# Expert rows in tiles of 32 tokens by 4 picks, indices and weights moved between partitions by products

## The chip, the cores and the metric

One core of one Trainium2 chip runs the whole program. The metric is device time in microseconds for one execution; less is better. All data is float32.

## The reference, cut to what matters

One layer of a hybrid network over 256 context tokens and 1024 latent tokens, D = 1024. Token mixing (gated MLP, pooling, retention) comes first. The change lies in the channel mixing, which looks up 128 experts for each token (8 heads by 16 picks):

```python
qp = (xt @ wq).reshape(t, PEER_HEADS, 2, PEER_DKEY // 2)
sc = jnp.einsum('thsk,hsnk->thsn', qp, subkeys)
top_s, top_i = lax.top_k(sc, PEER_TOPK)
...
best_s, best_p = lax.top_k(cand_s, PEER_TOPK)
expert = jnp.take_along_axis(cand_i, best_p, axis=-1)
g = jax.nn.softmax(best_s, axis=-1)
act = jax.nn.gelu(jnp.einsum('thkd,td->thk', u_tab[expert], xt))
y = jnp.einsum('thk,thkd->td', g * act, v_tab[expert])
```

Each expert is a row of `u_tab` and one of `v_tab`, 4 KB each, kept side by side in `in_peer` (8 KB). 1280 tokens by 128 picks are 163,840 rows, 1342 MB.

## The kernel before

The tokens are 10 chunks of 128. Two kinds of work are interleaved in one list of events, and each engine runs its part of the list in that order.

*The front* is everything but the expert rows, in stages: the retention scans and the pooling of the context, then of the latents; then, for groups of chunks (0: two, 1: two, 2: three, 3: three), a dense part (projections by weights streamed through the two buffers of `ring`, gates, output projection, the normed input h2) and a ranking part. There each chunk and pair of heads takes one `wq` event (query product, transposes, scores, on PE) and on DVE the events `topa`, `topb`, `topc` for each head of the pair: top 16 of each side, top 16 of the sums, then the expert numbers. The ranking goes pair by pair: pair 0 of every chunk of the group, then pair 1, and so on. Group 0's ranking is spread over the latent scans (two of its events behind each `hq`, `hk`, `hv` event).

*The rows* are 1280 row tiles, 128 for each chunk. A row tile holds 64 tokens by 2 picks on 128 partitions. POOL gathers its 128 rows of 8 KB into one of 8 slots (6 until group 0 is ranked) once the pair's indices are there and the slot is free (`row_free`). DVE multiplies the u half by h2 and sums (L1447), ACT makes the gelu, the weight and the weighted selection `lhs` (L953, L954, L958), PE multiplies `lhs` (64 columns) with the v half, 512 columns into each half of the PSUM partitions (L1178), and the slot is free. Inside a chunk the tiles go pair by pair, 16 of one half of the tokens (`g2`), 16 of the other. `h2R` holds h2 of the 64 tokens twice, for each half of a chunk. After a half's last tile DVE multiplies the sums by the gate (L1531) and adds them to the output rows (L1535).

DVE writes expert numbers and softmax weights straight into the rows' layout: the picks of a token that lies on one partition are spread over two, by 4 small instructions a head for the indices (L1500) and 8 a pair for the weights (L1515).

`Plan.merge` sets the order. It gives every front event a cost (the largest of its PE, ACT and DVE estimates), spreads the 128 tiles of a group's chunks evenly by cost from the point at which that group's rows may start to that of the next group (the last group at one tile for 2.9 us), and puts a tile behind an event when it is due and its pair is ready:

```python
while row + 1 <= due[n + 1] and self.ready[row_of(row)[0], row_of(row)[2]] <= n + 1:
```

What is not placed by the end of the front follows as the tail. PE runs a tile's product three tiles late, ACT one.

## Time and profile before

| | us |
|---|---|
| median of 3 runs | 4936.25 |
| lowest, highest | 4924.78, 4938.27 |
| the profiled execution | 4929.44 |
| its span, first to last instruction | 4927.7 |
| mean granted TensorE clock | 0.847 |

The profiled execution lies 6.8 us under the median, within the runs. The span is read by stage, since the mean shares mix stages with different bounds; the windows below are cut at the last scan update (1075), the last h2 of each group (1653, 2457, 3596) and the last index product of each ranking (1969, 2950, 4105, rounded to the instruction behind it).

### The profile page before, as it was taken

Reading aid. Unit: us, or ns where it says so; the run is one execution under the profiler, and the core shown is the slowest. Engines: PE = TensorE matmul, PEld = TensorE weight load, DVE = VectorE, ACT = ScalarE, POOL = GpSimd, SP = SyncE. Lnnn points to the kernel's source line nnn. Section 1 sums busy time; section 2 is a strip of 40 time slices with the busy share of each in tenths; the row PEclk is TensorE's granted clock in tenths of the full one; section 3 lists DMA queues with packets and bytes.
Section 4 is the critical chain, followed back from the end, with each engine's and each line's share of the span. In section 5 each row is a group of like instructions: output and inputs, shape, how many; then the busy total and the mean of one; then the engine's idle time right before and its main releaser. Section 6 shows DMA issues by size and latency. Waiting matters only on the chain. (4 is left out here: it accounts for less than half of the span.)

```text
span 4927.7 us, 44934 instructions
## 1 busy us (share of the span) xinstructions
PE 3968.5 (81%) x12301; PEld 1584.9 (32%) x12301; DVE 2747.1 (56%) x6701; ACT 1593.8 (32%) x4955; POOL 1616.5 (33%) x1312
## 2 busy tenths in 40 slices
PE   6999898999999865999876658988876755666666
PEld 4644355554434321344321213343322210111110
DVE  1112678433234499455569895545468996544544
ACT  4111244332122243323333333323343333333333
POOL 0000123221122232343333334344333334555554
PEclk8999999999999975999987769999977766666666
DMA  6644787878798987999999899999999878999998
GB/s 252 223 182 176 252 314 290 302 268 333 283 367 342 340 346 272 375 380 380 393 369 351 363 358 369 422 396 384 412 418 370 341 294 347 409 421 415 415 422 354
DMA packets 290059, 1687.33 MB, mean 342 GB/s; under 512 B 29136, under 2 KB 71184, under 8 KB 111120
## 3 DMA queue, kind: packets, MB, share of 16 engines
q0 software_dynamic: 184320, 1342.26, 68.8%
q1 hardware_dynamic: 97472, 318.79, 17.0%
q10 hardware_dynamic: 8016, 23.42, 1.5%
q8 instruction: 98, 1.61, 0.1%
q14 instruction: 153, 1.25, 0.1%
HBM read 1646.57 MB, written 37.78 MB: 342 GB/s over the span
## 5 line engine op out<-in xcount | busy, mean ns | idle before, releaser
L913 POOL DMA_INDIRECT slots<-in_peer,idxR x1280 | 1610.2, 1258 | 3257.8 <-PE ps L1178 2525.8
L1178 PE MATMUL ps<-slots,lhs 128*64 128x512 f32 x5120 | 1667.9, 765 | 818.3 <-ACT lhs L958 815.9
L1447 DVE CUSTOM_DVE_ANT_0 slots<-slots,h2R 128x1024 f32<-128x1024 f32 x1280 | 1540.2, 1224 | 814.8 <-issue 730.1
L1166 PE MATMUL ps<-ring,arena 128*128 128x512 f32 (+1 forms) x3996 | 1591.0, 553 | 28.8 <-DMA ring<-in_wq 22.2
L1166 PEld LDWEIGHTS ps<-ring,arena 128*128 128x128 f32 x3996 | 760.6, 195 | 884.2 <-issue 830.2
L1178 PEld LDWEIGHTS ps<-slots,lhs 128*64 128x64 f32 x5120 | 330.8, 158 | 2018.6 <-ACT lhs L958 1695.3
L953 ACT ACTIVATE gelus<-dots 128x1 f32<-128x1 f32 x1280 | 256.0, 200 | 1596.4 <-DVE dots L1447 1593.8
L958 ACT ACTIVATE lhs<-fold,wgts 128x64 f32<-128x64 f32 x1280 | 445.1, 348 | 41.9
L954 ACT ACTIVATE wgts<-gelus,gsmR 128x1 f32<-128x1 f32 x1280 | 377.1, 295 | 42.1
L1166 PE MATMUL ps<-ring,slots 128*128 128x512 f32 (+1 forms) x704 | 250.9, 518 | 0.4 <-DMA ring<-in_wz 0.4
L1166 PEld LDWEIGHTS ps<-ring,slots 128*128 128x128 f32 x704 | 134.0, 191 | 114.3 <-issue 105.9
L1118 ACT ACTIVATE tmp<-ps 128x512 f32<-128x512 f32 x60 | 35.8, 597 | 318.9 <-PE ps L1166 318.9
L1686 DVE SCALAR_TENSOR_TENSOR tmp<-tmp,ps 128x512 f32<-128x512 f32 x40 | 27.5, 688 | 194.7 <-ACT tmp L1123 194.7
L1166 PE MATMUL ps<-arena,ring 128*128 128x512 f32 x256 | 117.9, 615 | 10.6 <-DMA arena<-hT_scratch 10.6
L1447 DVE DVE_READ_ACCUMULATOR2_ANT dots<- 128x1 f32 x1280 | 104.9, 82 | 0.0
L1641 DVE TENSOR_TENSOR inb<-ps,inb 128x512 f32<-128x512 f32 x20 | 13.8, 691 | 144.6 <-PE ps L1166 139.0
L1667 DVE SCALAR_TENSOR_TENSOR arena<-tmp,arena 128x512 f32<-128x512 f32 x20 | 13.8, 692 | 137.9 <-ACT tmp L1118 137.9
L1123 ACT ACTIVATE tmp<-ps 128x512 f32<-128x512 f32 x40 | 23.9, 597 | 204.2 <-PE ps L1166 204.2
L953 ACT ACT_TABLE_LOAD x58 | 74.4, 1283 | 41.7 <-DVE dots L1447 41.0
L1142 ACT ACTIVATE arena<-ps 128x512 f32<-128x512 f32 x40 | 23.8, 596 | 193.0 <-PE ps L1166 193.0
L1515 DVE TENSOR_SCALAR gsmR<-es,rsum 64x8 f32<-64x8 f32 x320 | 74.2, 232 | 5.5
L1166 PEld LDWEIGHTS ps<-arena,ring 128*128 128x128 f32 x256 | 48.8, 196 | 80.8 <-issue 80.8
(194 smaller groups left out, 2340.4 us busy)
## 6 DMA issues: line engine op xcount, KB each, us to landing
ring<-in_whead SPq DMA_DIRECT2D x24, 2048.0 KB, 9.4
ring<-in_wa SPq DMA_DIRECT2D x24, 2048.0 KB, 9.6
ring<-in_wq SPq DMA_DIRECT2D x16, 2048.0 KB, 18.4
slots<-in_peer,idxR POOLq DMA_INDIRECT x1280, 11.4
ring<-in_wlate SPq DMA_DIRECT2D x16, 1024.0 KB, 7.5
ring<-in_wgc SPq DMA_DIRECT2D x16, 1024.0 KB, 9.4
ring<-in_wgb SPq DMA_DIRECT2D x8, 2048.0 KB, 10.0
ring<-in_wout SPq DMA_DIRECT2D x8, 2048.0 KB, 12.6
```

Source lines behind the costliest of these rows:

```text
L913: g.indirect_dma_start(out=slot(R), out_offset=None, in_=a["peer"], in_offset=bass.IndirectOffsetOnAxis(ap=idxR[:, p % KEEP, g2, col:col + ...
L953: st.link(A_(gelus[:, n:n + 1], dots[:, n:n + 1], ACT.Gelu_apprx_tanh))
L954: st.link(A_(wgts[:, n:n + 1], gelus[:, n:n + 1], ACT.Copy, scale=gsmR[:, p % KEEP, g2, col:col + 1]))
L958: A_(lhs[:, n, :], fold[:, :], ACT.Copy, scale=wgts[:, n:n + 1]).then_inc(s["w_done"], 1)
L1118: A_(tmp[:, ev.x % TMPS, :], bank(t), ACT.Tanh, scale=0.5).then_inc(freed[t % BANKS], 1)
L1123: A_(tmp[:, ev.x % TMPS, :], bank(t), ACT.Tanh, scale=0.5).then_inc(s["gate_done"], 1)
L1142: A_(qp[:, m % 2, :], bank(t), ACT.Copy).then_inc(freed[t % BANKS], 1)
L1166: done = mm(out, lhsT, rhs, start=n == 0, stop=n == len(pairs) - 1)
L1178: done = mm(ps[j * HALF:(j + 1) * HALF, g2, :], lhs[:, R % LHS, :], slot(R)[:, D + j * UW:D + (j + 1) * UW], start=start, stop=stop)
L1447: v.tensor_tensor_reduce(out=u, in0=u, in1=h2R[:, g2, :], scale=1.0, scalar=0.0, op0=ALU.mult, op1=ALU.add, accum_out=dots[:, R % LHS:R % ...
L1515: done = v.tensor_scalar(gsmR[i * HALF:(i + 1) * HALF, p % KEEP, g2, h * 8:h * 8 + 8], es[there, b, hd, :].rearrange("p (q i) -> p i q", i ...
L1686: v.scalar_tensor_tensor(out=gate, in0=gate, scalar=1.0, in1=bank(t), op0=ALU.add, op1=ALU.mult).then_inc(freed[t % BANKS], 1)
```

## The change

A row tile becomes 32 tokens by 4 picks. The product uses four column groups: `lhs` has 32 columns, and each of four products covers 256 columns of v and its own 32 PSUM partitions. The 64 tiles of a chunk's first half (64 tokens, quarters 0 and 1 by turns of 8 tiles) all come before those of the second half (quarters 2 and 3). `h2R` holds h2 of 32 tokens four times, so it is loaded four times for a chunk, and the sums are evacuated four times, by 1 + 4 instructions.

Expert numbers and weights go to a new buffer `vals`, on the partition of their token, by one instruction a head each. A new event `mv` multiplies slices of the identity with `vals` (16 products a pair), which puts every pick on its partition in PSUM; ACT copies the weights into `gsmR`. A new event `mw` lets DVE copy the indices into `idxR`. Only then may POOL gather for the pair. In the list `mv` stands behind the first `topc` of the next pair, `mw` behind the `topa` after that. Both are events of the ranking, so group 0's takes 8 instead of 6 places for a pair.

The planner has a pair ready at its `mw`, takes 2.8 instead of 3.3 us for each `top` event, and lets the rows of groups 2 and 3 start at the first chunk's pair 2 (was pair 1).

```diff
 def row_of(R):
-    p, rr = divmod(R, ROWS)
-    pair, g, qq = rr // 32, rr // 16 % 2, rr % 16
-    return p, g, pair, pair * 16 + qq, 2 * pair + qq // 8
+    p, n = divmod(R, ROWS)
+    g, pair = 2 * (n // HALF) + n // 8 % 2, n // 16 % 4
+    return p, g, pair, 8 * pair + n % 8, 2 * pair + n // PICKS % 2
...
+                    if m and hd == 0 and part == "c":
+                        self.moved(k, m - 1)
+                        yield
+                    if m and hd == 1 and part == "a":
+                        self.laid(k, m - 1)
+                        yield
...
-        starts = [self.ready[BASE[k], int(len(cs) > 2)] for k, cs in enumerate(GROUPS)] + [len(self.front)]
+        starts = [self.ready[BASE[k], 2 * (len(cs) > 2)] for k, cs in enumerate(GROUPS)] + [len(self.front)]
...
-                pool.wait_ge(s["idx_done"], 2 * pair_number(p, pair) + head % 2 + 1)
+                pool.wait_ge(s["idx_done"], pair_number(p, pair) + 1)
...
-                    for i in range(2):
-                        eng.dma_start(h2R[i * HALF:(i + 1) * HALF, ev.j, :],
-                                      h2d[ev.c][ev.j * HALF:(ev.j + 1) * HALF, :]).then_inc(h2R_in[ev.j], 16)
+                    for i in range(4):
+                        eng.dma_start(h2R[i * QT:(i + 1) * QT, ev.j % 2, :],
+                                      h2d[ev.c][ev.j * QT:(ev.j + 1) * QT, :]).then_inc(h2R_in[ev.j % 2], 16)
...
+                elif k == "mv":
+                    filled(eng, t)
...
+                    A_(gsmR[:, ev.p % KEEP, :, 8 * ev.j:8 * ev.j + 8], moved(t)[:, :, 1, :],
+                       ACT.Copy).then_inc(s["gsm_done"], 1)
...
-                for j in range(2):
-                    done = mm(ps[j * HALF:(j + 1) * HALF, g2, :], lhs[:, R % LHS, :],
-                              slot(R)[:, D + j * UW:D + (j + 1) * UW], start=start, stop=stop)
+                for j in range(4):
+                    done = mm(sums(g2)[j * QT:(j + 1) * QT, :], lhs[:, R % LHS, :],
+                              slot(R)[:, D + j * GW:D + (j + 1) * GW], start=start, stop=stop)
...
+                elif k == "mv":
+                    room(t)
+                    pe.wait_ge(s["val_done"], ev.z + 1)
+                    for g2 in range(4):
+                        for i in range(4):
+                            done = mm(bank(t)[i * QT:(i + 1) * QT, 4 * g2 * PICKS:4 * (g2 + 1) * PICKS],
+                                      ident[:, g2 * QT:(g2 + 1) * QT],
+                                      vals[:, ev.z % 2, i, :, :, :].rearrange("p v h s -> p (v h s)"),
+                                      start=True, stop=True)
...
-                for g2 in range(2):
-                    for i in range(2):
-                        here = picked[g2 * HALF:(g2 + 1) * HALF, :, :].rearrange("p v (q i) -> p v i q", i=2)
-                        done = v.scalar_tensor_tensor(
-                            out=idxR[i * HALF:(i + 1) * HALF, p % KEEP, g2, ev.h * 8:ev.h * 8 + 8],
...
+                here = picked.rearrange("p v (i s) -> p v i s", i=4)
+                st.step(v.scalar_tensor_tensor(out=vals[:, ev.z % 2, :, 0, ev.j, :], in0=here[:, 0, :, :],
+                                               scalar=float(NK), in1=here[:, 1, :, :],
...
                 for hd in range(2):
-                    for g2 in range(2):
-                        for i in range(2):
...
+                    st.step(v.tensor_scalar(vals[:, b, :, 1, hd, :],
...
-                    for j in range(2):
-                        part = yb[here, j * UW:(j + 1) * UW]
-                        st.step(v.tensor_tensor(part, part, ps[j * HALF:(j + 1) * HALF, g2, :], ALU.add))
+                    for j in range(4):
+                        part = yb[here, j * GW:(j + 1) * GW]
+                        st.step(v.tensor_tensor(part, part, sums(g2)[j * QT:(j + 1) * QT, :], ALU.add))
...
+                elif k == "mw":
+                    dve.wait_ge(s["gsm_done"], ev.z + 1)
...
+                    st.link(v.tensor_copy(idxR[:, ev.p % KEEP, :, 8 * ev.j:8 * ev.j + 8], moved(ev.y)[:, :, 0, :]))
+                    dve.sem_inc(s["idx_done"], 1)
```

How many row tiles stand in each stage of DVE's written order:

| stage | before | changed |
|---|---|---|
| latent scans (with group 0's ranking) | 121 | 120 |
| dense 1 (with the latents' pooling) | 114 | 115 |
| ranking 1 | 79 | 71 |
| dense 2 | 136 | 123 |
| ranking 2 | 161 | 134 |
| dense 3 | 196 | 199 |
| ranking 3 | 153 | 167 |
| tail | 320 | 351 |

The first place is PE in the third head of the latent scans, before (`arena` by `ring` are the v products, `ring` by `arena` the q and k products or the other way round, `slots,lhs` the row tiles, 2 a tile):

```order
L1166 MATMUL ps<-arena,ring 128x512 x8
L1178 MATMUL ps<-slots,lhs 64x512 x4
L1166 MATMUL ps<-ring,arena 128x256 x16
L1178 MATMUL ps<-slots,lhs 64x512 x2
L1166 MATMUL ps<-ring,arena 128x256 x16
L1178 MATMUL ps<-slots,lhs 64x512 x4
```

The same head in the changed order, tiles of 4 products (L1219), moves as `vals,ident`:

```order
L1207 MATMUL ps<-arena,ring 128x512 x16
L1255 MATMUL ps<-vals,ident 32x16 x16
L1207 MATMUL ps<-arena,ring 128x512 x16
L1207 MATMUL ps<-ring,arena 128x256 x32
L1255 MATMUL ps<-vals,ident 32x16 x16
L1207 MATMUL ps<-ring,arena 128x256 x16
L1219 MATMUL ps<-slots,lhs 32x256 x148
L1207 MATMUL ps<-ring,arena 128x256 x16
```

One or two tiles stood behind each dense tile; now none stands from the second head's scans to here, and 37 follow at once. The same place of the second head has `x64`, 16 tiles, and one of the first head `x20`, 5 tiles. Each burst stands directly behind the `mw` of the pair that its first tile needs.

The second place is the end of PE's list, before:

```order
L1178 MATMUL ps<-slots,lhs 64x512 x20
L1386 MATMUL ps<-ident,arena 128x128 x4
L1397 MATMUL ps<-arena 128x128 x4
L1178 MATMUL ps<-slots,lhs 64x512 x16
L1397 MATMUL ps<-arena 128x128 x4
L1178 MATMUL ps<-slots,lhs 64x512 x672
```

and changed:

```order
L1448 MATMUL ps<-arena 128x128 x4
L1219 MATMUL ps<-slots,lhs 32x256 x12
L1255 MATMUL ps<-vals,ident 32x16 x16
L1219 MATMUL ps<-slots,lhs 32x256 x24
L1255 MATMUL ps<-vals,ident 32x16 x16
L1219 MATMUL ps<-slots,lhs 32x256 x16
L1255 MATMUL ps<-vals,ident 32x16 x16
L1219 MATMUL ps<-slots,lhs 32x256 x1420
```

Before, PE's last front product is the last pair's scores, with 336 tiles behind it, while DVE still ranks; now it is the last move, at DVE's own position less three tiles, with 355 behind it.

## Rows read from the trace of the kernel before

**Rows 1.** The page: span, busy line of PE, slices of PEclk, DMA and GB/s.
```profile
span 4927.7 us, 44934 instructions
...
PE 3968.5 (81%) x12301; PEld 1584.9 (32%) x12301; DVE 2747.1 (56%) x6701; ACT 1593.8 (32%) x4955; POOL 1616.5 (33%) x1312
...
PEclk8999999999999975999987769999977766666666
...
DMA  6644787878798987999999899999999878999998
...
GB/s 252 223 182 176 252 314 290 302 268 333 283 367 342 340 346 272 375 380 380 393 369 351 363 358 369 422 396 384 412 418 370 341 294 347 409 421 415 415 422 354
```

**Rows 2.** Windows: length; PE, PEld, DVE, ACT, POOL busy; PEclk, DMA share, GB/s.
```profile
563.00:1075.00 512.00, 467.78 (x1821) 270.62 (x1822) 330.96 (x936) 201.32 (x663) 135.96 (x120) 0.95 0.81 293
1075.00:1653.00 578.00, 569.46 (x1648) 244.69 (x1646) 201.22 (x342) 140.77 (x430) 129.44 (x115) 0.99 0.86 332
1653.00:1969.00 316.00, 195.11 (x568) 65.46 (x564) 260.05 (x832) 105.08 (x310) 90.84 (x79) 0.72 0.83 312
1969.00:2457.00 488.00, 472.44 (x1456) 200.12 (x1456) 240.82 (x414) 157.79 (x487) 186.09 (x138) 0.99 0.97 380
2457.00:2950.00 493.00, 322.38 (x960) 102.80 (x960) 416.19 (x1267) 179.20 (x560) 173.18 (x153) 0.74 0.92 363
2950.00:3596.00 646.00, 568.23 (x1742) 223.88 (x1742) 340.53 (x606) 222.52 (x701) 261.09 (x203) 0.95 0.98 396
3596.00:4105.00 509.00, 331.44 (x960) 102.14 (x960) 430.01 (x1314) 185.14 (x569) 181.23 (x155) 0.71 0.88 344
4105.00:4900.00 795.00, 538.95 (x1252) 84.16 (x1252) 399.55 (x649) 272.31 (x951) 444.51 (x311) 0.65 1.01 415
```

**Rows 3.** The page's costliest groups: the expert rows' three.
```profile
L913 POOL DMA_INDIRECT slots<-in_peer,idxR x1280 | 1610.2, 1258 | 3257.8 <-PE ps L1178 2525.8
L1178 PE MATMUL ps<-slots,lhs 128*64 128x512 f32 x5120 | 1667.9, 765 | 818.3 <-ACT lhs L958 815.9
L1447 DVE CUSTOM_DVE_ANT_0 slots<-slots,h2R 128x1024 f32<-128x1024 f32 x1280 | 1540.2, 1224 | 814.8 <-issue 730.1
```

**Rows 4.** Groups of DVE by form: index, weights, evacuation, a cast.
```profile
L1515 DVE TENSOR_SCALAR gsmR<-es,rsum 64x8 f32<-64x8 f32 x320 | 74.2, 232 | 5.5
...
L1500 DVE SCALAR_TENSOR_TENSOR idxR<-picked 64x8 uint32<-64x8 f32 x320 | 51.7, 162 | 6.1
...
L1535 DVE TENSOR_TENSOR yb<-yb,ps 64x512 f32<-64x512 f32 x40 | 27.4, 686 | 1.3
...
L1531 DVE TENSOR_TENSOR ps<-ps,gt 128x512 f32<-128x512 f32 x20 | 13.9, 697 | 49.5 <-PE ps L1178 49.3
...
L1487 DVE CAST abf<-ab 128x32 f32<-128x32 uint32 x80 | 14.5, 182 | 2.7
```

**Rows 5.** Timeline of PE in dense 3: start, length, what, entries.
```profile
2999.71 7.13 PE L1166 MATMUL ps<-ring,arena 128*128 128x512 f32 x16
3006.77 2.79 PE L1178 MATMUL ps<-slots,lhs 128*64 128x512 f32 x12
```

**Rows 6.** Timeline of PE in the first stage: 32-column weights; 2-column products.
```profile
153.36 1.93 PE L1206 MATMUL ps<-ring,slots 128*32 128x256 f32 x32
...
165.64 0.95 PE L1213 MATMUL ps<-sel,slots 128*128 128x2 f32 x8
```

**Rows 7.** DMA issues: count, KB each, median us to landing.
```profile
slots<-in_peer,idxR POOLq DMA_INDIRECT x1280, 11.4
...
h2R<-h_scratch ACTq DMA_DIRECT2D x40, 256.0 KB, 8.6
```

**Rows 8.** The chain of waits in the tail: start, us, what.
```profile
4110.32 5.51 DMA slots<-in_peer,idxR
...
4148.58 2.00 PE ps L1178 x4
...
4151.34 13.59 DMA slots<-in_peer,idxR
```

More of the change, by code:

```diff
@@ L37 @@
 HALF = P // 2
+QT = P // 4
+PICKS = TOP // 4
 SLOTS = 8
@@ L478, in row @@
         p = (R - PE_LAG) // ROWS
-        for g in range(2):
+        for g in range(4):
             if R >= PE_LAG and R - PE_LAG == last_row(p, g):
                 self.events.append(Event("ev", p=p, c=ORDER[p], j=g))
-                if g:
+                if g == 3:
                     self.tail = [Event(kind, p=p, c=ORDER[p]) for kind in ("fa", "fb", "fc")]
@@ L486, in row, with quarter_before @@
         self.spare(R + 1, n)
+    @staticmethod
+    def quarter_before(p, g):
+        return (p, g - 2) if g >= 2 else (p - 1, g + 2)
     def spare(self, rows, n):
         for p in range(NC):
-            for g in range(2):
+            for g in range(4):
                 if (p, g) not in self.loaded and self.prepared[p] <= n and (
-                        p == 0 or rows >= last_row(p - 1, g) + 2):
+                        h2_load(p, g) == 1 or rows >= last_row(*self.quarter_before(p, g)) + 2):
                     self.loaded.add((p, g))
@@ L699, in scans_by, with sums, moved @@
             return before(G_, HEADS * CC, HEADS * (NC - CC)) + len(STAGES[G_]) * h
+        def sums(g):
+            return ps[:, g % 2, 0:GW]
+        def moved(t):
+            return bank(t)[:, 0:4 * 4 * PICKS].rearrange("p (g v n) -> p g v n", g=4, v=2)
         def slot(R):
@@ L882, in _ @@
                                     base=0, pattern=[[-1, P]], channel_multiplier=1))
-            st.link(g.affine_select(out=fold[:, :], in_=fold[:, :], compare_op=ALU.not_equal, fill=1.0,
-                                    base=0, pattern=[[-1, HALF]], channel_multiplier=1))
-            st.step(g.affine_select(out=fold[:, :], in_=fold[:, :], compare_op=ALU.not_equal, fill=1.0,
-                                    base=-HALF, pattern=[[-1, HALF]], channel_multiplier=1))
+            for b in range(4):
+                st.link(g.affine_select(out=fold[:, :], in_=fold[:, :], compare_op=ALU.not_equal, fill=1.0,
+                                        base=-QT * b, pattern=[[-1, QT]], channel_multiplier=1))
             for b in range(4):
@@ L903, in _ @@
             for R in range(NR):
-                p, g2, pair, col, head = row_of(R)
+                p, g2, pair, col, _ = row_of(R)
                 if R == 0:
@@ L1446, in row @@
                 u = slot(R)[:, 0:D]
-                v.tensor_tensor_reduce(out=u, in0=u, in1=h2R[:, g2, :], scale=1.0, scalar=0.0,
+                v.tensor_tensor_reduce(out=u, in0=u, in1=h2R[:, g2 % 2, :], scale=1.0, scalar=0.0,
                                        op0=ALU.mult, op1=ALU.add,
@@ L1511, in softmax @@
                 for hd in range(2):
-                    for g2 in range(2):
-                        for i in range(2):
-                            there, h = slice(g2 * HALF, (g2 + 1) * HALF), 2 * pair + hd
-                            done = v.tensor_scalar(
-                                gsmR[i * HALF:(i + 1) * HALF, p % KEEP, g2, h * 8:h * 8 + 8],
-                                es[there, b, hd, :].rearrange("p (q i) -> p i q", i=2)[:, i, :],
-                                rsum[there, hd:hd + 1], None, ALU.mult)
-                done.then_inc(s["gsm_done"], 1)
+                    st.step(v.tensor_scalar(vals[:, b, :, 1, hd, :],
+                                            es[:, b, hd, :].rearrange("p (i s) -> p i s", i=4),
+                                            rsum[:, hd:hd + 1], None, ALU.mult))
+                st.settle()
+                dve.sem_inc(s["val_done"], 1)
             for ev in plan.events:
```

94 lines of the change are left out of this document (52 added, 42 removed).

## The prediction

> **What bounds the kernel now.** I read the page first. PE is busy 81% of the span and the DMA engines stand at 8 or 9 tenths in nearly every slice after the first tenth, while the clock line is at full speed in some slices and at 6 tenths at the end [rows 1]. So no one engine bounds the whole, and I cut the span into eight stages at the program's own borders: the scans of the latents, then a dense part (projections, gates, output) and a ranking part (query products and top-16) for each of groups 1, 2, 3, then the tail in which nothing but expert rows is left. The windows show a different bound in each [rows 2]. The scans (563 to 1075) and the dense part of group 1 (1075 to 1653) are PE's: 468 of 512 us and 569 of 578 us busy. The dense part of group 2 is PE's with DMA close behind (472 of 488, share 0.97). The dense part of group 3 is DMA's (0.98, PE 568 of 646). The three rankings are DVE's: 260 of 316, 416 of 493 and 430 of 509 us, with PE idle a third of the time at a clock of 0.71 to 0.74. The tail (4105 on) is DMA's alone: share 1.01 at 415 GB/s, 311 gathers in 795 us, so 2.55 us for one row tile. The best slice of the whole page is 422 GB/s [rows 1], which I take as the ceiling. Each tile costs PE 4 MATMULs, DVE 1.20 us (1540.2 / 1280) and one gather of 1.05 MB (128 rows of 8 KB, 2.5 us at 420 GB/s), and POOL's gathers wait mostly for PE's product, that is for a free slot [rows 3].
>
> **The product of a tile.** Between dense tiles at full clock three tiles take 2.79 us less the overlap of the last, 0.92 us each, beside 7.13 us for a 16-MATMUL dense tile [rows 5]. Afterwards a tile is 4 column groups of 256 columns over 32 weight columns. This form stands in the trace: 32 MATMULs of 128*32 by 256 in 1.93 us, or 0.48 us for eight [rows 6]. So a tile saves 0.43 us of PE at full clock, and about 1 us at half clock (1.98 us for one in the tail's chain, [rows 8]). It is worth time only where PE is the bound.
>
> **The move between partitions.** Per pair of heads, DVE gives up 8 index products of 162 ns and 8 scalings of 232 ns [rows 4], 3.2 us. It gains 2 + 2 such on 128 partitions (16 elements each, 0.16 to 0.23 us as their like of before) and one cast of about 0.2 us (182 ns for 32 elements), 1.0 us: -2.2 us for each of 40 pairs. Evacuation: before, per chunk 2 x (697 + 2 x 686) ns = 4.1 us [rows 4]; after, 4 x (1 + 4) instructions at some 0.42 us for 256 columns (half the columns, a little fixed cost), 8.4 us, so +4.3 us per chunk. PE gains 32 entries (16 products, two passes) per pair. The nearest rows give 0.06 us (32-column weights, [rows 6]) or 0.12 us (8 with 128x128 weights in 0.95 us): 1.9 to 3.8 us, doubled at half clock. I take 2, nearer in shape to the first. The Trainium skill ("TensorEngine Tiling (Array Packing)", Instruction Overhead) says a matmul has about 60 cycles of overhead, so that one column costs as much as 60; at 2.4 GHz that would be 0.8 us for the 32, less than both rows, and the sum would fall by about 1 us a pair. The 2-column products of [rows 6] took 0.12 us, well over it. DVE meets the result one ranking step (3 us) later; I allow 0.6 us of waiting a pair.
>
> **h2 copies.** Four loads of 512 KB for a chunk instead of two: +1.05 MB, 2.5 us of DMA a chunk. They must land within 8 tiles (20 us at the tail's pace); they took 8.6 us [rows 7], so no stall.
>
> **Order of the tiles.** This is the larger part. A chunk's first half now needs all four pairs after 48 tiles, where the old order needed the fourth after 96. The table of counts shows what the planner makes of it, and I cost each stage with it.
>
> *Scans, 121 to 120 tiles.* PE shows bursts of 5, 16 and 37 tiles in a row, each straight behind the index copy that its pair needs. POOL can't fetch them ahead, and PE, in order, can do nothing else. A burst runs at the gather's 2.5 us, 145 us for 58 tiles, plus a first landing each. In the trace the shortest that the tail's chain shows is 5.5 us and the median of all 11.4 [rows 7, 8]; with an empty queue I take 8, so 24. PE's head start (5 us each) and its lag of three tiles come off, 38. That leaves 131 us of stopped dense work. Sum: dense 468 - 121 x 1.02 = 345 (0.92 us, 1.98 in the tenth of the time that the clock of 0.95 leaves at half), moves 8 x 2, the other 62 tiles x 0.48 = 30, idle 35 of the 44 before, bursts 131: 557 against 512, **+45**. (The Trainium skill, "DMA: Bandwidth & Descriptors", Anatomy of one DMA, fits a DMA from GpSimd as 2.0 us + bytes / 436e3, an estimated 4.4 us for a lone gather; by it the three first landings would come 11 us cheaper. No row shows one that short.) Bounds: +10 (PE far ahead of DVE) to +85 (first landings of 14 us, half clock after each).
>
> *Dense 1, 114 to 115.* -114 x 0.43 = -49; DMA would go from 0.86 to 0.94, so nearly all counts: **-45** (-25 to -50).
>
> *Ranking 1, 79 to 71.* DVE -8 x 1.20 = -10, -8 x 2.2 = -18, evacuation +3, waits +5. But tiles 272 and 288 stand directly behind their index copy and 256 and 304 close behind: four cold gathers, 10 + 10 + 4 + 4 = +28. **+8**.
>
> *Dense 2, 136 to 123.* PE would lose 66 us, DMA only 13 x 2.5 - 3 = 30 of 473: DMA is next at 443, so 450 for 488, **-38**.
>
> *Ranking 2, 161 to 134.* -27 x 1.20 = -32, -12 x 2.2 = -26, evacuation +5, waits +7, and of 77 us of idle some 10 fewer as the DMA share falls: **-56**.
>
> *Dense 3, 196 to 199.* DMA-bound: +3 x 2.5, copies +4: **+11**.
>
> *Ranking 3, 153 to 167.* +14 x 1.20 = +17, -26, +5, +7, and idle +7 as DMA goes from 0.88 to 0.94: **+10**.
>
> *Tail, 320 to 351.* 31 x 2.55 = 79, copies 2.7 x 2.5 = 7: **+86**. Product and scaling get shorter there, but hide behind the saturated DMA.
>
> Sum: 45 - 45 + 8 - 38 - 56 + 11 + 10 + 86 = **+21 us**. The profiled execution took 4929.4 us (span 4927.7), near the middle of the runs; on their median of 4936.25 that gives 4957. What a measurement can tell from no change is about 0.3%, 15 us. The likeliest case's own range is 4930 to 5000.
>
> **Rivals.**
> *Round trip, not bandwidth.* The tail's chain goes gather 13.6 us, DVE, ACT, product 2.0, POOL [rows 8]; eight slots in a loop of 20 us give exactly 2.5 us a tile. If the loop is the limit and not the engines, a product shorter by 1 us gives 2.42, the tail 351 x 2.42 = 849 for 823 (+26 instead of +86), dense 2 and 3 gain what PE saves, -65 and -60 instead of -38 and +11. Together 4957 - 60 - 27 - 71 = 4799; half of it, 4878. For it: 8 x 2.5 = 20. Against: the share of 1.01 and equal 415 to 422 GB/s in stages with other traffic. Chance 0.2, nearly all faster.
> *The move is a meeting point.* PE must wait for DVE's softmax at each move, ACT and DVE for PE; 40 times. If each costs the stage's bound 3 us instead of 0.6, +96 us: 5053. With all else at no change it makes the kernel slower by 15 us from 0.4 us a pair on. For it: the scans have PE 91% and DVE 65% busy, so both are often needed; against: PE is idle a third of the rankings [rows 2]. Chance 0.2, slower.
> *Bursts hidden.* If PE has fallen far behind DVE when a burst comes, gathers land while it catches up: scans +10, ranking 1 -10, so 4957 - 35 - 18 = 4904. Chance 0.15: faster 0.08, same 0.05, slower 0.02.
> *As forecast.* 0.45: its range makes it slower 0.26, same 0.16, faster 0.03.
> Together faster 0.31, same 0.21, slower 0.48. The range of all leaves out the ends of the first two rivals: 4868 to 5040.
>
> **What would show it.** Eight products of a tile near 0.48 us beside dense tiles; dense 1 near 533 us; two stretches of about 45 and 95 us in the scans in which PE runs only tiles while DMA is at 1.0; the last index copy some 60 us earlier than 4101, then 351 tiles at 2.55 us. Wrong, if the tail's pace falls under 2.48 us (first rival), if DVE's wait before the index cast is over 1 us in the mean (second), or if the scans take no longer than 525 us (third).

## The result

The changed kernel takes 5023.93 us (median of 4 runs, 5019.72 to 5033.86); the kernel before took 4930.51 us beside it (4 runs). The ratio is 1.0192, with a 95% interval of 1.0167 to 1.0216: 93 us slower. The forecast was 21 us slower, with a range of 4868 to 5040. The direction was right and the size was not. Below, medians of different kernels are subtracted from each other: the kernel before was run again beside every experiment and its medians lie between 4929.5 and 4931.4 us, while single runs lie up to some 15 us off the median of their kernel. A difference of medians under some 10 us is not told from noise. Ratios leave out the one slow run among all of these, 5187 us of the kernel of experiment 1.

The page of the changed kernel, to be read against [rows 1]: span, PE's busy line, the clock, the DMA engines' share and what they moved.

```profile
span 5024.7 us, 57832 instructions
...
PE 3424.3 (68%) x18701; PEld 1560.3 (31%) x18701; DVE 2704.9 (54%) x6401; ACT 1562.6 (31%) x4990; POOL 1415.6 (28%) x1314
...
PEclk8999898689999975899977579898866655555555
DMA  6545564688899977799988989999999979999998
GB/s 253 216 183 186 180 238 160 251 324 310 343 371 382 381 274 289 313 397 399 411 324 340 377 338 422 383 381 410 405 407 383 372 299 408 408 408 420 409 409 359
```

PE is busy 544 us less, and the span is 97 us longer. Slices 5 to 8 show where: the DMA engines stand at 4 to 6 tenths, with one slice of 160 GB/s, where they stood at 7 and 8 before. The windows give the size. They are cut where DVE starts the last scan update, the last h2 of a group and the last index copy of a ranking (scans, dense 1, ranking 1, and so on to the tail):

```profile
563.00:1184.00 621.00, 457.01 (x2517) 277.31 (x2516) 316.97 (x863) 194.81 (x660) 144.83 (x125) 0.83 0.67 249
1184.00:1725.70 541.70, 521.40 (x2111) 241.05 (x2108) 207.81 (x361) 138.39 (x436) 127.42 (x116) 0.99 0.93 360
1725.70:2038.70 313.00, 139.82 (x1051) 61.13 (x1050) 233.00 (x730) 95.70 (x289) 72.73 (x69) 0.66 0.71 276
2038.70:2485.80 447.10, 422.12 (x1936) 195.60 (x1928) 231.31 (x404) 144.89 (x450) 155.44 (x126) 0.98 0.99 397
2485.80:2935.30 449.50, 235.65 (x1785) 95.71 (x1786) 382.05 (x1155) 165.99 (x518) 143.40 (x131) 0.68 0.89 349
2935.30:3580.20 644.90, 514.60 (x2536) 224.40 (x2536) 326.90 (x565) 205.26 (x676) 239.88 (x202) 0.90 0.98 393
3580.20:4098.60 518.40, 262.08 (x2048) 102.53 (x2052) 429.77 (x1237) 195.47 (x623) 180.84 (x165) 0.67 0.93 367
4098.60:5024.60 926.00, 380.77 (x2836) 71.43 (x2828) 462.94 (x777) 300.86 (x1080) 344.35 (x347) 0.50 0.99 402
```

The windows of [rows 2] can't be set against these: their border behind ranking 2 stands at 2950, while the last index product of that ranking starts at 2967.0, and the borders behind the other rankings are 7 and 3 us late. Cut as above, the kernel before has:

```profile
563.00:1074.20 511.20, 466.98 (x1820) 270.33 (x1820) 330.48 (x935) 200.58 (x659) 135.96 (x120) 0.95 0.81 293
1074.20:1651.40 577.20, 568.65 (x1646) 244.45 (x1643) 200.13 (x342) 140.48 (x433) 129.44 (x115) 1.00 0.86 331
1651.40:1962.30 310.90, 190.81 (x555) 64.00 (x554) 256.99 (x820) 101.10 (x300) 89.97 (x78) 0.72 0.84 317
1962.30:2455.90 493.60, 478.33 (x1474) 202.12 (x1472) 244.34 (x428) 161.73 (x495) 186.23 (x138) 0.99 0.96 376
2455.90:2967.00 511.10, 332.96 (x982) 105.33 (x983) 433.35 (x1316) 187.32 (x585) 180.23 (x160) 0.73 0.92 361
2967.00:3595.10 628.10, 556.93 (x1719) 221.30 (x1718) 323.57 (x557) 214.63 (x675) 254.78 (x198) 0.96 0.99 398
3595.10:4101.60 506.50, 332.16 (x963) 102.19 (x960) 427.68 (x1304) 184.12 (x568) 179.70 (x154) 0.71 0.88 345
4101.60:4927.60 826.00, 551.27 (x1280) 85.94 (x1280) 414.21 (x680) 283.01 (x981) 447.89 (x313) 0.64 0.99 404
```

| stage | before | after | change | forecast |
|---|---|---|---|---|
| scans | 511 | 621 | +110 | +45 |
| dense 1 | 577 | 542 | -35.5 | -45 |
| ranking 1 | 311 | 313 | +2 | +8 |
| dense 2 | 494 | 447 | -46.5 | -38 |
| ranking 2 | 511 | 449.5 | -61.6 | -56 |
| dense 3 | 628 | 645 | +17 | +11 |
| ranking 3 | 506.5 | 518 | +12 | +10 |
| tail | 826 | 926 | +100 | +86 |

Every stage but three (scans, dense 1, tail) lies within 9 us of its forecast, and the scans alone miss by 65.

The DMA column says the same in one number. Length times what the share lacks to 1 is 97 us of idle DMA in the scans before (511 x 0.19) and 205 us now (621 x 0.33): 108 us more, nearly the whole of what the scans lost. POOL shows it too: before the larger burst no gather is issued for 103.66 us, until DVE's index copy is there.

```profile
825.00:925.00 100.00, 85.84 (x389) 59.18 (x382) 53.36 (x188) 25.38 (x83) 0.00 (x0) 0.93 0.19 69
...
926.24 0.94 POOL L948 DMA_INDIRECT slots<-in_peer,idxR  x1 [103.66 <-DVEq L1794]
```

PE's timeline in the scans: start of the first dense tile and its wait, a move, a later dense tile at full clock, then the ends of the larger burst (the middle is left out), and last one row tile in dense 3.

```profile
597.04 9.50 PE L1207 MATMUL ps<-arena,ring 128*128 128x512 f32 x16 [33.00 <-DMA arena<-hT_scratch]
...
625.10 0.45 PE L1255 MATMUL ps<-vals,ident 128*32 128x16 f32 x32 [2.92 <-DVEq L1562]
...
645.17 7.17 PE L1207 MATMUL ps<-ring,arena 128*128 128x256 f32 x32
...
922.76 8.83 PE L1207 MATMUL ps<-ring,arena 128*128 128x256 f32 x32
931.51 1.07 PE L1219 MATMUL ps<-slots,lhs 128*32 128x256 f32 x16
...
1023.47 1.08 PE L1219 MATMUL ps<-slots,lhs 128*32 128x256 f32 x8 [2.13 <-ACT lhs L993]
1025.96 1.08 PE L1219 MATMUL ps<-slots,lhs 128*32 128x256 f32 x8 [1.41 <-ACT lhs L993]
1026.97 9.62 PE L1207 MATMUL ps<-ring,arena 128*128 128x256 f32 x32
...
3043.31 0.64 PE L1219 MATMUL ps<-slots,lhs 128*32 128x256 f32 x8 [0.46 <-ACT lhs L993]
```

From 931.5 to 1027.0 PE has nothing but 37 tiles, most of them 2.49 us apart, each a product of 1.08 us at half clock behind a wait. The 16 tiles of the other burst stop it from 791.4 to 828.6. A tile's eight products take 0.64 us where they stand alone and 1.07 us for two, so the forecast's 0.48 is about right for tiles in a row (before, three took 2.79, [rows 5]). The dense tile behind the burst takes 9.62 us, where the same 32 entries took 7.17 earlier.

The groups by form that answer to [rows 3] and [rows 4] (tile product, move, evacuation, scaling, index product, index cast), and the page's row of the h2 copies, for [rows 7]:

```profile
L1219 PE MATMUL ps<-slots,lhs 128*32 128x256 f32 x10240 | 1045.3, 509 | 1072.7 <-ACT lhs L993 1066.7
L1255 PE MATMUL ps<-vals,ident 128*32 128x16 f32 x1280 | 24.3, 212 | 334.3 <-DVEq L1562 334.3
...
L1578 DVE TENSOR_TENSOR yb<-yb,ps 32x256 f32<-32x256 f32 x160 | 66.8, 417 | 5.1
L1558 DVE TENSOR_SCALAR vals<-es,rsum 128x16 f32<-128x16 f32 x80 | 14.9, 233 | 1.4
L1549 DVE SCALAR_TENSOR_TENSOR vals<-picked 128x16 f32<-128x16 f32 x80 | 13.9, 174 | 2.8
L1793 DVE CAST idxR<-ps 128x32 uint32<-128x32 f32 x40 | 7.4, 186 | 3.5 <-ACT gsmR L1192 2.6 <-DVE ti L1507 0.2
```

```profile
h2R<-h_scratch ACTq DMA_DIRECT2D x160, 128.0 KB, 7.6
```

The small operations cost what their like of before suggested. The wait is not where I looked for it: DVE waits 2.6 us in all for the result of a move (0.07 us a pair), but PE waits 334 us in all for DVE's softmax (L1562 of the changed kernel), 8.4 us a move; in the scans it is 3.3 us at each of seven.

The chain of waits in the tail answers to [rows 8]:

```profile
4182.31 1.13 PE ps L1219 x8
...
4184.19 17.65 DMA slots<-in_peer,idxR
...
4220.29 1.13 PE ps L1219 x8
```

The product fell from 2.00 to 1.13 us, and the gather that follows takes longer by more than that (13.59 us before). The DMA engines' share between 4120 and 4900 is 1.01 as before; POOL issues 297 gathers in these 780 us, one in 2.63 us (before 311 in 795, one in 2.56, [rows 2]).

### The profile page after: what moved, and what is told of

The parts are those of the page before. It is cut to its first block, busy times and chain, and to the rows that moved or that the text cites. A ratio compares the mean times of both kernels' runs of the same rounds, so it can differ in the third digit from the quotient of the medians.

```text
span 5024.7 us, 57832 instructions
## 1 busy us (share of the span) xinstructions
PE 3424.3 (68%) x18701; PEld 1560.3 (31%) x18701; DVE 2704.9 (54%) x6401; ACT 1562.6 (31%) x4990; POOL 1415.6 (28%) x1314
## 4 chain that ended last, share of the span: by engine, by line
PE 39%; DMA 30%; DVE 14%; issue 10%; ACT 4%; SPq 1%; POOL 1%; DVEq 0%; ACTq 0%; POOLq 0%
PE ps L1207 31%; DMA slots<-in_peer,idxR 26%; PE ps L1219 5%; DVE slots L1498 4%; ACT wgts L989 1%; DMA ring<-in_wq 1%; ACT lhs L993 1%; DMA ring<-in_mlat 1%; DVE ti L1507 1%; POOL slots L948 1%; DVE ti L1504 1%; DVE hot L1539 1%; DVE hot L1543 1%; DVE picked L1545 1%; ACT gelus L988 1%
## 5 line engine op out<-in xcount | busy, mean ns | idle before, releaser
L948 POOL DMA_INDIRECT slots<-in_peer,idxR x1280 | 1408.9, 1101 | 3554.4 <-PE ps L1219 2523.2
L1219 PE MATMUL ps<-slots,lhs 128*32 128x256 f32 x10240 | 1045.3, 509 | 1072.7 <-ACT lhs L993 1066.7
L1207 PE MATMUL ps<-ring,arena 128*128 128x512 f32 (+1 forms) x3996 | 1635.4, 566 | 48.8 <-DMA ring<-in_wq 22.9
L1207 PEld LDWEIGHTS ps<-ring,arena 128*128 128x128 f32 x3996 | 781.3, 200 | 840.1 <-issue 766.5
L1219 PEld LDWEIGHTS ps<-slots,lhs 128*32 128x32 f32 x10240 | 259.6, 125 | 1830.0 <-ACT lhs L993 1641.4
L993 ACT ACTIVATE lhs<-fold,wgts 128x32 f32<-128x32 f32 x1280 | 411.3, 321 | 41.9
L1255 PE MATMUL ps<-vals,ident 128*32 128x16 f32 x1280 | 24.3, 212 | 334.3 <-DVEq L1562 334.3
L1255 PEld LDWEIGHTS ps<-vals,ident 128*32 128x32 f32 x1280 | 21.2, 148 | 362.3 <-issue 362.3
## 6 DMA issues: line engine op xcount, KB each, us to landing
slots<-in_peer,idxR POOLq DMA_INDIRECT x1280, 12.9
```

The source lines that it names most:

```text
L948: g.indirect_dma_start(out=slot(R), out_offset=None, in_=a["peer"], in_offset=bass.IndirectOffsetOnAxis(ap=idxR[:, p % KEEP, g2, col:col + ...
L993: A_(lhs[:, n, :], fold[:, :], ACT.Copy, scale=wgts[:, n:n + 1]).then_inc(s["w_done"], 1)
L1207: done = mm(out, lhsT, rhs, start=n == 0, stop=n == len(pairs) - 1)
L1219: done = mm(sums(g2)[j * QT:(j + 1) * QT, :], lhs[:, R % LHS, :], slot(R)[:, D + j * GW:D + (j + 1) * GW], start=start, stop=stop)
```

## The experiments

Three theories stood after the result, to be told apart by runs. **Starved gathers**: tile 48 of chunk 0 needs the chunk's fourth pair, ranked seventh of eight, so the gathers stand idle and then come in bursts. **Meeting point**: each move makes PE wait for DVE, whatever the order. **Price of the tail**: the planner's two numbers push 34 tiles into a stage where each costs 2.5 us. All ratios are against the kernel before, run beside each. Code is cut to the lines that matter, with `...` where some are left out.

### 1. The same kernel without the bursts

```
+    if k == 0:
+        return 4 * p + pair
...
-            pair, i = divmod(m, n)
+            pair, i = ranked(k, m)      # group 0: m % 4, m // 4
...
-                found = bank(ev.y) if ev.g else score[:, ev.i, :]
+                found = bank(ev.y) if ev.g else score[:, ev.h // 2 * len(GROUPS[0]) + ev.p, :]
```

> The changed kernel, with group 0 alone ranked chunk by chunk (all four pairs of chunk 0, then those of chunk 1) instead of pair by pair; the number of tiles in each stage stays as it is. Theory 1 (starved gathers): the loss sits in the latent scans, because tile 48 of chunk 0 needs that chunk's last pair, which is ranked seventh of eight; the gathers stand idle and then come in bursts of 16 and 37 tiles, in which PE does no dense work for 133 us. With the pairs in the new order no burst is left, the scans shrink from 621 to about 520 us (133 us less, 53 tiles by 0.6 us more), and the kernel takes about 4925 us (4905 to 4945). Theory 2 (meeting point): the loss is PE's waiting for DVE's softmax at the 40 moves, 334 us in all; these stay, so the time stays within 15 us of 5024.

Measured: 4939.13 us, ratio 1.0019 (1.0005 to 1.0033), 85 us less. The windows of its scans and its tail:

```profile
563.00:1093.50 530.50, 433.10 (x2512) 276.03 (x2512) 311.22 (x850) 195.04 (x662) 147.36 (x123) 0.90 0.79 291
...
4003.30:4928.30 925.00, 381.29 (x2836) 71.95 (x2828) 463.13 (x777) 300.75 (x1080) 344.76 (x347) 0.50 0.99 403
```

The scans became 90.5 us shorter and no other stage moved by 5: the bursts are shown to be the main cause, with their size. The DMA share of the scans is back from 0.67 to 0.79.

### 2. The move alone

The kernel before with `vals`, `mv` and `mw`, and 4 products for a move instead of 16 (2 halves by 2 picks):

```
+                    for g2 in range(2):
+                        for i in range(2):
+                            done = mm(bank(t)[i * HALF:(i + 1) * HALF, 32 * g2:32 * (g2 + 1)],
+                                      ident[:, g2 * HALF:(g2 + 1) * HALF], ...
```

> The kernel before (tiles of 64 tokens by 2 picks, its products, its copies and its tile order) with the move alone: indices and weights go through vals and 4 products with the identity, and only then may the pair be gathered. Theory 1 (starved gathers): the old order of tiles needs a chunk's fourth pair only after 96 tiles, so no burst arises; what is left is the wait at the moves (23 us in the scans) and the later first gather (17 us), less DVE's shorter writes: 4940 to 4970 us. Theory 2 (meeting point): most of the 93 us come with the move itself: 4990 us or more.

Measured: 4919.33 us, ratio 0.9976 (0.9967 to 0.9985), 12 us faster than before: both theories expected it slower. Its windows for the scans and ranking 2:

```profile
563.00:1113.10 550.10, 476.48 (x1880) 277.06 (x1880) 312.61 (x849) 200.20 (x668) 138.09 (x125) 0.92 0.78 284
...
2494.10:2988.90 494.80, 328.35 (x1097) 112.11 (x1097) 416.32 (x1208) 196.08 (x617) 188.08 (x164) 0.78 0.96 382
```

The move costs the scans 39 us (550 for 511) and gives more than that back later: over the whole span DVE is busy 92 us less (2747.1 in [rows 1], 2654.6 now). The rankings, where DVE is the bound, are 31 us shorter together (ranking 2 495 for 511); dense 3 and the tail are 21 shorter, and they also hold some 8 tiles fewer.

### 3. A product left out, and products of half the columns

```
-                for j in range(2):
+                for j in range(2 if start or stop else 1):
```

> The kernel before, with the second 512 columns of a tile's product left out (but in a half's first and last tile), so that a tile costs PE about 0.46 us instead of 0.92, as the changed one does; half of the summed columns is wrong. If the forecast's terms for the product are right, the scans lose about 50 us, dense 1 about 45 and dense 2 about 38, and dense 3 and the tail nothing: 4790 to 4820 us. If tiles are fetched no faster anywhere, since the gathers bound those stages too, less than 50 us: above 4880. If the tail is a round trip, its pace falls under 2.5 us a tile and the time under 4770.

Half of the summed columns is left out here. Measured: 4928.77 us, ratio 0.9996 (0.9986 to 1.0007), no change. That is not an answer to the question, as its timeline in dense 3 shows: a tile is now 2 entries instead of 4, and three tiles take what they took in [rows 5].

```profile
2997.79 2.79 PE L1178 MATMUL ps<-slots,lhs 128*64 128x512 f32 x6
3000.51 7.13 PE L1166 MATMUL ps<-ring,arena 128*128 128x512 f32 x16
```

Two products of 64 weight columns, into different halves of the partitions, run side by side, so leaving one out takes nothing off. (The Trainium skill, "TensorEngine Tiling (Array Packing)", Available Configurations, lists 128x64 as two tiles; the trace agrees, 2.79 us for three row tiles with 12 entries and with 6.) What is left to cut is the columns that stream. So the second try halves those:

```
+                    w = UW if start or stop else UW // 2
+                    done = mm(ps[j * HALF:(j + 1) * HALF, g2, 0:w], lhs[:, R % LHS, :],
+                              slot(R)[:, D + j * UW:D + j * UW + w], start=start, stop=stop)
```

> The kernel before with both products of a tile over 256 columns instead of 512 (but in a half's first and last tile), so half of the summed columns is wrong. The run without the second product showed that the two products of a tile run side by side in PE's column groups (2.79 us for three tiles either way), so this one, not that, gives a tile of about 0.48 us. By the forecast's terms the scans lose about 50 us, dense 1 about 45, dense 2 about 38, dense 3 and the tail nothing: 4790 to 4820 us. If the tiles' time on PE is cover for gathers in every stage, 4880 to 4930 us. If the tail is a round trip, under 4770.

Half of the summed columns is left out here too. Measured: 4849.37 us, ratio 0.9836 (0.9822 to 0.9849), 82 us faster. Its scans, dense 1 and dense 2:

```profile
563.00:1047.10 484.10, 423.69 (x1820) 271.38 (x1820) 326.77 (x925) 198.35 (x658) 144.29 (x120) 0.94 0.83 307
1047.10:1591.60 544.50, 526.37 (x1645) 246.29 (x1644) 200.02 (x343) 140.72 (x433) 130.75 (x115) 0.99 0.91 352
...
1902.10:2366.40 464.30, 429.71 (x1472) 201.76 (x1470) 245.66 (x427) 161.82 (x495) 165.87 (x138) 0.98 0.98 399
```

Against the kernel before, cut in the same way, that is 27, 33 and 29 us less, and nothing elsewhere; the tail took 824 us against 826. So the cost of a tile is in the columns, and a shorter product is worth 82 us, all in three stages, not the 130 or so that I expected. The tail is no round trip.

### 4. The planner's numbers alone

```
-        starts = [self.ready[BASE[k], int(len(cs) > 2)] for k, cs in enumerate(GROUPS)] + [len(self.front)]
+        starts = [self.ready[BASE[k], 2 * (len(cs) > 2)] for k, cs in enumerate(GROUPS)] + [len(self.front)]
```

and 2.8 us instead of 3.3 for a ranking event, both in the kernel before.

> The kernel before, with the planner's part alone: the rows of groups 2 and 3 start at the first chunk's pair 2, and a ranking event counts 2.8 us instead of 3.3. Its list has 34 tiles more in the tail and 34 fewer in ranking 2. By the forecast's own terms (1.2 us of DVE for a tile less in a ranking, 2.5 us for one more in a stage bound by the gathers) that is about +45 us: 4975 us. If the gathers' idle time does not grow, no change: within 15 us of 4930.

Measured: 4980.43 us, ratio 1.0109 (1.0089 to 1.0128), 49 us slower. The sum of the forecast's prices (45) holds, and so does the tail's: 913.5 us against 826, 2.5 us for each of 35 tiles more. The stages between do not hold as closely: ranking 2 fell by 55 us, 1.7 for each tile less and not 1.2, while dense 3 and ranking 3 took 21 us more each. Then the reverse, the old numbers in the changed kernel without bursts in the scans:

> The changed kernel with group 0 ranked chunk by chunk (4939 us) and the planner's two numbers of before (rows of groups 2 and 3 from the first chunk's pair 1 on, 3.3 us for a ranking event). Its tail has 37 tiles fewer; in return bursts of 9, 8, 15, 38 and 11 tiles stand in the rankings, each behind the index copy of its pair. If the planner's numbers cost here what they cost in the order of before (49 us for 34 tiles), the time is about 4890 us. If a burst in a ranking costs what it costs in the scans (the gather's 2.5 us a tile, less the 1.2 us that DVE gives for it anyway, so about 81 x 1.3 = 105 us and some cold landings, against 94 saved in the tail), 4935 to 4970 us.

Measured: 5024.35 us, ratio 1.0196 (1.0182 to 1.021), 85 us slower than with the new numbers and worse than either expectation. The tail gained 98 us, but ranking 1 and dense 2 together took 817 us against 756, ranking 2 and dense 3 together, where the bursts of 15 and 38 tiles stand, 1206 against 1098, and ranking 3 took 20 more. So the new numbers cost 49 us in the old order of tiles and are worth 85 in this one: they belong to the order, and their price can't be taken from the change by itself.

### 5. Half of the copies

The changed kernel, with two of the four copies left out (the wait for them counts two as well):

```
-                    for i in range(4):
+                    for i in range(4 if ev.p == 0 and ev.j < 2 else 2):
```

> The changed kernel with only two of the four copies of a quarter's h2 loaded from chunk 0's second half on (the dot products of the other half of the partitions are wrong): 10 MB less. If the bytes of the copies count where the DMA engines are the bound (all stages from dense 2 on), about 10.0 MB at 422 GB/s, 24 us less, most of it: 5000 to 5010 us. If the copies are hidden, 5024 us as before.

Measured: 4996.31 us, ratio 1.014 (1.0125 to 1.0156), 28 us less for 10 MB less, which at 422 GB/s would be 24. The copies' bytes are paid at about the full rate. The profiled pair lies 39 us apart: 15 in the tail (910.8 for 926 us; 303 gathers in the 780 us that held 297), 12 in dense 3 and ranking 3, and 11 in the scans, where I had not looked for any.

### 6. The move one ranking event later

In the kernel of experiment 1 (4939 us, no bursts):

```
-                    if m and hd == 0 and part == "c":
+                    if m and hd == 1 and part == "a":
                         self.moved(k, m - 1)
...
-                    if m and hd == 1 and part == "a":
+                    if m and hd == 1 and part == "b":
                         self.laid(k, m - 1)
```

> The changed kernel with group 0 ranked chunk by chunk (4939 us) and each move one ranking event later: the products with the identity behind the next pair's second topa, the index copy behind the topb after it. PE then waits less for DVE's softmax (about 3 us less at each of 40 moves), and each pair may be gathered 3 us later. If PE's waits at the moves cost the kernel time (rival of the meeting point), it gets faster by 15 us or more: 4925 us or less. If they are cover that PE has anyway, the time stays within 10 us of 4939.

Measured: 4887.78 us, ratio 0.9914 (0.99 to 0.9927): 51 us less than without it. PE's waits for DVE's softmax at the moves in the scans (us in all, times, longest), before this edit:

```profile
PE ps L1264 <- DVEq L1571: 34.2, 7, 7.5
```

and with it:

```profile
PE ps L1264 <- DVEq L1571: 4.0, 1, 4.0
```

The window of its scans:

```profile
563.00:1030.00 467.00, 411.14 (x2504) 261.91 (x2504) 311.55 (x856) 194.84 (x659) 146.37 (x124) 0.96 0.89 328
```

The scans fell by 63.5 us: 30 in these waits, 10 in PE's waits for DVE's scan products, and 22 in PE's busy time for the same work, as the granted clock rose from 0.90 to 0.96. So such waits were paid twice here: once as idle time, and again as busy time at a lower granted clock. Not all of it reached the end: dense 1 (551.8 for 541.5 us) and ranking 1 (321.6 for 310.9) took 21 us more. In the changed kernel with its bursts the same edit gives little:

> The changed kernel with its own order (group 0 ranked pair by pair, bursts of 16 and 38 tiles) and only each move one ranking event later. In the order without bursts that gave 51 us, 63 of them in the scans. If the waits at the moves and the bursts are two causes that add up, the same comes here: 5024 less 40 to 55, 4970 to 4985 us. If PE, stopped by bursts anyway, meets DVE's numbers later in any case, so that one hides the other, less than 20 us: above 5004.

Measured: 5015.51 us, ratio 1.0171 (1.0157 to 1.0185), 8 us less, within the noise. The expectation for this size was that the bursts hide the waits at the moves. The profile says otherwise: these waits were there with the bursts (first line) and went with the edit (second).

```profile
PE ps L1255 <- DVEq L1562: 23.1, 7, 5.2
...
PE ps L1255 <- DVEq L1562: 4.0, 1, 4.0
```

The scans fell by 30 us, of which 12 in PE's busy time, but the granted clock of the stage stayed at 0.83, and ranking 1 (10.5), dense 3, ranking 3 and the tail gave 20 us back. Why so much was given back is not shown.

In the kernel of experiment 1 again, one more event later:

> The kernel of the later move (group 0 ranked chunk by chunk, 4888 us) with each move one more ranking event later: products behind the second topb, index copy behind the second topc. PE still waits 171 us at 23 moves there, nearly all in the rankings, 4 us in the scans. If waits in the rankings cost nothing, the time stays within 10 us of 4888; if they do, 15 us or more faster.

Measured: 4911.51 us, ratio 0.9955 (0.994 to 0.997), 24 us worse, which neither side expected. PE's waits at the moves fell from 171 to 84 us, all of that in the rankings, and brought nothing; the scans took 481 us for 467. Why they did is open.

And the move one event later in the tile and order of the kernel before, that is in the kernel of experiment 2:

> The kernel before with the move alone (4919 us), each move one ranking event later. Its scans took 550 us against 511 without the move. If the place of the move costs that, the scans fall by 30 to 50 us and the time is 4870 to 4890 us, faster than both kernels. If only the order without bursts gained by it, the time stays within 10 us of 4919.

Measured: 4887.53 us, ratio 0.9916 (0.9902 to 0.9929), 32 us less than with the move at its first place; the scans took 504.7 us for 550.1.

### 7. Where the later move costs, and the start of the scans

The first gathers now come when the latents' hT is loaded, and PE waits 33 us for it instead of 10.6. One line, added to the kernel of experiment 6 (4888 us), makes the gathers wait for the load:

```
                     pool.wait_ge(s["hT_out"], 16 * (NC - CC))
+                    pool.wait_ge(s["hl_in"], 16 * (NC - CC))
```

> The kernel of the later move (4888 us), with the first gather of all waiting for the latents' hT to be in. At the start of the scans PE waits 32 us for that load (10.6 us in the kernel before), beside which the first six gathers now run, since the first pair's indices come 25 us later than they did. If the gathers' traffic stretches the load, PE starts 10 to 15 us earlier and 5 to 15 us come off: 4873 to 4883 us. If the load is late for another reason (its start behind the last query product), no change, or some us slower for the later gathers.

Measured: 4883.14 us, ratio 0.9903 (0.9889 to 0.9917). PE's wait fell from 32.3 to 17.0 us, so 15 of the 22 us more came from the gathers beside the load. The time is 5 us less, which the noise covers:

```profile
PE ps L1217 <- DMA arena<-hT_scratch: 17.0, 1, 17.0
```

Next the later move in group 0 alone, the rankings of groups 1 to 3 as they were, and the gathers free again:

> The changed kernel with group 0 ranked chunk by chunk and each move one ranking event later in group 0 alone; the rankings of groups 1 to 3 keep the changed kernel's place of the move. If the later move costs the rankings the gathers' later start, ranking 1 falls back from 321 to 311 us and the tail from 930 to 925, and the time is 4865 to 4880 us, under the 4888 of the kernel with all moves later. If the scans only hand their time on, 4888 us within 8.

Measured: 4871.54 us, ratio 0.9882 (0.9863 to 0.9901), 16 us less: ranking 1 312.8 us for 321.6, the tail 925.7 for 929.7. In the scans the place of the move is PE's time; in the rankings PE waits for nothing that counts, and one event later is only a later gather. With both edits, in the tile of before and in the changed one:

> The kernel before (its tile, order and planner) with the move alone, one ranking event later in group 0 alone, and the first gather waiting for the latents' load. Against the kernel with all moves later (4888 us) ranking 1 should fall by 10 us and the start of the scans by some 5: 4870 to 4880 us. If neither counts, 4888 us within 8.

Measured: 4859.99 us, ratio 0.9857 (0.9836 to 0.9877).

> The kernel of the later move in group 0 alone (changed tile, chunk by chunk), with the first gather waiting for the latents' load. PE waited 15 us less for that load where this was tried alone, and 5 us came of it. If that adds to the rankings' gain, 4860 to 4875 us; if the gathers given up at the start are missed later, as much as without it or more.

Measured: 4859.18 us, ratio 0.9853 (0.9835 to 0.9871), scans 453.8 us:

```profile
563.00:1016.80 453.80, 412.58 (x2504) 264.38 (x2504) 312.11 (x858) 195.50 (x659) 147.91 (x124) 0.97 0.92 338
```

The line for the load is worth 12 us here (4859 for 4872, with no run of one among those of the other), 8 of them in the scans. Both kernels beat the kernel before by 71 and 72 us and cannot be told from each other: with a move of good place the tile of 32 tokens by 4 picks brings nothing over that of 64 by 2. By the single measurements its product is worth 82 us, and the planner's numbers (49) and the copies (28) take 77, which leaves 5 us: the parts add up here.

## Why the forecast was right in direction and wrong in size

**The step that failed is the sum of the scans**, +45 for a measured +110: 65 of the 72 us by which the whole forecast was short. The mechanism was right, a burst behind each late index copy, and so was the size of this term: 131 us, measured 95.5 + 37.2 = 133 for the two large bursts, and without them the scans took 90 us less. Part of that is luck. The term was 58 tiles at 2.5 us, with 24 us for first landings and less 38 for PE's head start and lag. All three bursts took 140 us, so neither correction shows in its size, and they nearly cancelled (no wait in the larger burst is over 3.5 us; no row stood behind the head start of 5 us). The terms beside it were too small, each for a reason that the profile shows:

| term of the scans | forecast | measured |
|---|---|---|
| bursts | 131 | 133 |
| dense work, transposes, scans | 345 | 360 |
| the other tiles | 30 | 40 |
| moves | 16 | 27 |
| idle | 35 | 61 |
| sum | 557 | 621 |

(Measured: busy 457.0, of which the tiles 93.2, 53.3 of that in the two bursts, the small burst being among the other tiles; moves 7 x 0.5 busy and 23.1 of waiting; other waits 33.0, 19.0 and 9.1 for hT, the scan products and `lhs`.)

- *Moves*: I allowed DVE 0.6 us for meeting the result and PE 2 us for the products. The products take 0.45 to 0.63 us, less than both of my rows gave, and less than the 0.8 of the estimate beside them; but PE waits 3.3 us a move for DVE's softmax. I asked who waits for the result, not what the move itself waits for.
- *Dense work and tiles*: I took the clock of before for what is left. The granted clock is 0.53 in the larger burst, where PE is busy 38 of 95 us, and the dense tile behind it still takes 9.62 us for 7.17; over the scans it is 0.83 for 0.95. Experiment 1, without the bursts, has 24 us less of busy time for the same work.
- *Idle*: the first gather of all starts at 563.5 us instead of 525.5, since its pair must be moved first, so the first gathers run beside the load of hT, and PE waits 22 us more for it; experiment 7 shows 15 of these to come from the gathers, and the load is issued 4.6 us later than before. The forecast priced the order of tiles and no transfer beside them.

**The tail**, +100 for +86: POOL issues 34 gathers more in it (347 for 313) instead of 31, and the copies cost 15 us there instead of 7.

**The product**: dense 1 -35.5 and dense 2 -46.5 for -45 and -38. The saving is real, 82 us over all by the half-column run, and DMA-bound stages give nothing back, as said. In dense 1 PE's busy time fell by 47 us as forecast (568.7 to 521.4), but its idle time grew by 12: it now waits 7 us for weight loads, for which it did not wait before.

**The rankings**, +2, -61.6 and +12 for +8, -56 and +10, and **dense 3**, +17 for +11: right within 6 us. What the four cold gathers that I charged to ranking 1 cost was not told apart; its DMA share is 0.71 for 0.83.

**The rivals.** *Round trip*: fallen. A product shorter by 0.9 us in the tail (1.98 to 1.08) left its pace at 2.63 us, and the half-column run left its tail at 824 us. *Bursts hidden*: fallen, PE stood in them for 140 us. *Meeting point*: this is a second, smaller cause that the forecast held for a rival with a chance of its own, while it adds to the bursts. DVE's wait before the index cast, by which I meant to tell it, is 0.07 us; the wait is PE's. Its place costs 51 us in the order without bursts and 32 in that of before (4919 to 4888). With the bursts it is 8, though the waits at the moves in the scans fall from 23.1 to 4.0 us there too; why so little of it reaches the end stays open.

Taken apart: the move 12 us faster, the shorter product 82 faster, the planner's numbers 49 slower (each against the kernel before), the copies 28 and the bursts 85 (each against the changed kernel). Their sum is 68 slower for 93 measured; 25 us are left that the parts cost together and not alone. The 49 us are those of the old order of tiles, so this is an account and not a proof. The rest points at the place of the move. Where that is the better one and the gathers wait for the load, product, planner's numbers and copies, added to the move alone (4860), give 4855 us for 4859 measured, a rest of 4 within the noise (experiment 7). And the move's place costs 51 us with the short tiles and 32 with the long ones, which is 19 of the 25; how the tile makes this difference is not shown.

## What to carry to other kernels

When a tile is turned so that its first use needs more of what comes late, look at which piece of the producer's order is now needed first, and turn the producer too: ranking chunk by chunk in group 0 gave back 85 of 93 us with the same instructions in another order. (Whether it would have helped the kernel before, which had no bursts, was not tried.) Where an engine is put between two others (produce on DVE, move on PE, take on DVE), price its wait for the producer in the stage in which it is the bound, and place it one step behind where the producer is expected to be; the same step later costs where that engine has time. And in a kernel bound by its transfers, add up the idle time of the DMA engines by stage: here it gave the loss of the worst stage in one subtraction. Before you subtract stages of two kernels, cut both at the same instruction: one border 17 us off in the rows of before shifted as much between two stages.

## What the runs showed of the hardware that was not expected

- Two products of 128x64 weights by 512 columns into different halves of the PSUM partitions take the time of one: three tiles 2.79 us with 12 entries and with 6. To take work off PE, shorten the columns that stream: at 256 the same tiles took 0.65 us alone and 1.08 us for two.
- 32 entries of 128x32 weights by 16 columns took 0.45 us in a row, 0.014 us each; they went to the four quarters of the partitions in turn.
- Waits of up to 7.5 us between dense tiles (34 us at the moves and 15 at the scan products, 4 and 5 after the edit) went with 22 us more of PE's busy time for the same work: the granted clock of the scans was 0.90 with them and 0.96 without.
- Three gathers of 1.05 MB each, issued after POOL had issued none for 104 us, landed in 5.8, 6.9 and 8.0 us; the median of all is 12.9.
- Loads of the latents' hT (8 x 512 KB) were issued over 27.07 us where gathers ran beside them, over 11.69 us in the kernel before, and over 11.07 us where the gathers were made to wait for them.
